# Half of the first shift of an adaLN block: summed on VectorE over transposed rows instead of on TensorE

## The reference

```python
def rms_norm(x, g):
    y = xf * lax.rsqrt(jnp.mean(xf * xf, axis=-1, keepdims=True) + NORM_EPS)
    return (y * g.astype(jnp.float32)).astype(x.dtype)

def adaln(cond, w, b):
    return jnp.split(jax.nn.silu(cond) @ w + b, 6, axis=-1)

def modulate(h, shift, scale):
    return h * (1 + scale) + shift

mx = adaln(cond_x, ada_w[i], ada_b[i])
mc = adaln(cond_c, ada_w[i], ada_b[i])
hx = modulate(rms_norm(x, norm1_g[i]), mx[0], mx[1])
hc = modulate(rms_norm(h_ctx, norm1_g[i]), mc[0], mc[1])
```

## Time and profile before

| | |
|---|---|
| median of 3 timed runs | 1277.91 us |
| the three runs | 1277.8, 1277.91, 1280.22 us |
| span of the profiled execution | 1280.4 us (no other time of it is given) |
| TensorE busy | 1187.3 us, 93% |
| VectorE busy | 744.2 us, 58% |
| ScalarE busy | 510.0 us, 40% |
| POOL busy | 410.8 us, 32% |
| mean granted clock of TensorE | 0.952 |

### The profile page before, as it was taken

The page is one execution under the profiler, slowest core; times in us unless marked ns, Lnnn a source line. Parts: engine busy times, 40 slices in busy tenths (PEclk is TensorE's granted clock), DMA queues, the critical chain, the costliest instruction groups (busy, mean ns, idle before and its releaser), DMA issues.

```text
span 1280.4 us, 17087 instructions
## 1 busy us (share of the span) xinstructions
PE 1187.3 (93%) x6196; PEld 945.7 (74%) x6196; DVE 744.2 (58%) x1082; ACT 510.0 (40%) x858; POOL 410.8 (32%) x185
## 2 busy tenths in 40 slices
PE   6889889897999999999998999997889898999999
PEld 1468653375788888778886788897556587999999
DVE  1688885557598889844114222244467765655544
ACT  2623433533423222322223445463756434544433
POOL 0243210032465555654442433474744200000000
PEclk9889987898999999999998999997989889999999
DMA  9353441033355555654332232343100035455566
GB/s 367 149 187 132 148 132 50 1 110 121 104 192 183 194 185 177 211 171 164 91 101 66 83 98 83 98 164 100 50 1 1 1 103 161 155 190 181 172 180 176
DMA packets 50874, 167.44 MB, mean 131 GB/s; under 512 B 5248, under 2 KB 6400, under 8 KB 50560
## 3 DMA queue, kind: packets, MB, share of 16 engines
q1 hardware_dynamic: 50816, 166.67, 39.7%
HBM read 165.60 MB, written 1.05 MB: 130 GB/s over the span
## 4 chain that ended last, share of the span: by engine, by line
PE 34%; issue 31%; POOL 18%; DVE 10%; DMA 3%; ACT 2%; POOLq 0%; SPq 0%; DVEq 0%; ACTq 0%
POOL wlo L774 18%; PE bank L1253 17%; DVE junk L828 4%; PE bank L1448 2%; PE bank L1262 2%; PE bank L1243 2%; PE bank L1567 2%; PE bank L1556 1%; PE bank L1275 1%; PE bank L1423 1%; DMA xT<-in_x_in 1%; PE bank L1336 1%; PE bank L1651 1%; PE bank L1603 1%; PE bank L1621 1%
## 5 line engine op out<-in xcount | busy, mean ns | idle before, releaser
L774 POOL TENSOR_TENSOR wlo<-raw,whi 128x1024 fp32r<-128x1024 f32 (+2 forms) x141 | 359.0, 2556 | 544.4 <-ACT whi L465 544.3
L1253 PE MATMUL bank<-hhi,whi 128*128 128x256 f32 (+1 forms) x1128 | 381.1, 338 | 3.1 <-POOL wlo L774 2.4
L1253 PE MATMUL bank<-hlo,whi 128*128 128x256 f32 (+1 forms) x1128 | 377.7, 335 | 0.0
L1253 PE MATMUL bank<-hhi,wlo 128*128 128x256 f32 (+1 forms) x1128 | 376.8, 334 | 0.0
L465 ACT ACTIVATE whi<-raw 128x1024 fp32r<-128x1024 f32 (+2 forms) x231 | 224.8, 980 | 202.1 <-DMA raw<-in_w_fo 91.8
L828 DVE SCALAR_TENSOR_TENSOR junk<-aring,csil 128x1024 f32<-128x1024 f32 x144 | 272.6, 1893 | 21.4 <-DMA aring<-in_ada_t 16.4
L1253 PEld LDWEIGHTS bank<-hhi,whi 128*128 128x128 f32 x1128 | 214.1, 190 | 27.5 <-issue 4.4
L1253 PEld LDWEIGHTS bank<-hhi,wlo 128*128 128x128 f32 x1128 | 212.9, 189 | 24.1
L1253 PEld LDWEIGHTS bank<-hlo,whi 128*128 128x128 f32 x1128 | 212.9, 189 | 22.2
L807 DVE TENSOR_TENSOR wlo<-raw,whi 128x1024 fp32r<-128x1024 f32 (+2 forms) x90 | 100.4, 1117 | 88.0 <-ACT whi L465 87.9
L1253 PE MATMUL bank<-ahi,whi 128*128 128x512 f32 (+1 forms) x352 | 118.9, 338 | 1.3 <-DVE scr L920 1.3
(11 more groups left out here) (191 smaller groups left out, 1457.7 us busy)
## 6 DMA issues: line engine op xcount, KB each, us to landing
raw<-in_w_fi SPq DMA_DIRECT2D x88, 512.0 KB, 3.7
aring<-in_ada_t SPq DMA_DIRECT2D x80, 512.0 KB, 3.8
raw<-in_w_in SPq DMA_DIRECT2D x55, 512.0 KB, 3.8
raw<-in_w_out SPq DMA_DIRECT2D x24, 512.0 KB, 4.3
raw<-in_w_fo SPq DMA_DIRECT2D x32, 384.0 KB, 3.1
raw<-in_w_fo SPq DMA_DIRECT2D x32, 320.0 KB, 3.0
ada<-in_ada_w SPq DMA_DIRECT2D x4, 2048.0 KB, 16.4
xT<-in_x_in SPq DMA_DIRECT2D x1, 2048.0 KB, 17.8
```

The costliest lines, as they stand in the source:

```text
L774: nc.gpsimd.tensor_tensor(wlo[:, s, 0:w], raw[:, s, 0:w], whi[:, s, 0:w].bitcast(F32), ALU.subtract).then_inc(lo_ready, 1)
L1253: ins = mm(dst, w[:, s, j * P:(j + 1) * P], xx[:, k0_ + j], start=first and j == 0 and o == 0, stop=last and j == n - 1 and o == 2)
```

## The change

Three of the four row groups remain on TensorE: both halves of the scale and the low half of the shift. The high half of the shift (512 outputs) is made on VectorE in the manner of the later adaLN units: four tiles `shift_w` of 128 outputs by 1024 inputs are loaded transposed (512 KB each, from a new input `ada_s`), and eight multiply-and-sum instructions, two for each tile, write to `asum[:, 4:8]`. They stand on VectorE's list behind the bias of row 1 and the gain, and before the bias of row 0 and the norm. Since they need the Silu of the conditioning rows, these are loaded right behind x, and ScalarE makes their Silu right behind the squares, before the first row copy. The norm's column sums stand behind group 1 instead of group 2; the high parts of chunks 0 and 1 stand behind the last row copy instead of before it. `add_bias` now takes the column of the bias and the number of tiles.

```diff
@@ the sync queue @@
-            for n in range(4):
+            for n in range(3):
                 src = ada_w[1 - n // 2, :, (n % 2) * 512:(n % 2 + 1) * 512].rearrange("(k p) n -> p k n", p=P)
                 sp.dma_start(ada0[:, n], src).then_inc(ada0_in[n], 16)
...
                 if n == 1:
                     sp.dma_start(xT[:, :, :], x_in).then_inc(x_landed, 16)
+                    sp.dma_start(csil[:, :, :], crow).then_inc(crow_in, 16)
+            for t in range(4):
+                sp.dma_start(shift_w[:, t, :], ada_s[t]).then_inc(shift_in[t], 16)
...
-            sp.dma_start(csil[:, :, :], crow).then_inc(crow_in, 16)
@@ ScalarE @@
-            for n in range(4):
+            act.wait_ge(crow_in, 16)
+            nc.scalar.activation(csil[:, :, :], csil[:, :, :], ACT.Silu).then_inc(crow_silu, 1)
+            for n in range(3):
                 act.wait_ge(ada0_rows, n + 1)
                 nc.scalar.activation(rows0[0:2, n, :], bank[n][0:2, :], ACT.Copy).then_inc(rows_out, 1)
-                if n == 2:
+                if n == 1:
                     norm_std(0, HALVES)
-                    act.wait_ge(crow_in, 16)
-                    nc.scalar.activation(csil[:, :, :], csil[:, :, :], ACT.Silu).then_inc(crow_silu, 1)
-                    hi(0)
-                    hi(1)
+            hi(0)
+            hi(1)
             norm(0, HALVES)
@@ VectorE @@
             norm_rstd(0, HALVES)
-            for n, row in enumerate((1, 0)):
-                dve.wait_ge(ada0_sum, n + 1)
-                add_bias(mod[:, row], bank[4 + n][:, 0:16].rearrange("p (k c) -> p k c", c=2), row)\
-                    .then_inc(mods_ready, 1)
-            gains(0, 2)
+            dve.wait_ge(ada0_sum, 1)
+            add_bias(mod[:, 1], bank[4][:, 0:16].rearrange("p (k c) -> p k c", c=2), PV_ADAB + KT, KT)\
+                .then_inc(mods_ready, 1)
+            gains(0, 1)
+            dve.wait_ge(crow_silu, 1)
+            for t in range(4):
+                dve.wait_ge(shift_in[t], 16)
+                for c in range(2):
+                    n = 2 * t + c
+                    if n:
+                        dve.wait_ge(shift_dot, n)
+                    vec.scalar_tensor_tensor(out=junk[:, :], in0=shift_w[:, t, :], scalar=1.0, in1=csil[:, c, :],
+                                             op0=ALU.mult, op1=ALU.mult, accum_out=asum[:, 4 + t, c:c + 1])\
+                        .then_inc(shift_dot, 1)
+            dve.wait_ge(ada0_sum, 2)
+            add_bias(mod[:, 0, 0:4], bank[5][:, 0:8].rearrange("p (k c) -> p k c", c=2), PV_ADAB, 4)
+            dve.wait_ge(shift_dot, 8)
+            add_bias(mod[:, 0, 4:8], asum[:, 4:8, :], PV_ADAB + 4, 4).then_inc(mods_ready, 1)
             norm(0, HALVES)
@@ TensorE @@
-                if n % 2:
+                if n:
                     ins.then_inc(ada0_sum, 1)
 
-            for n in range(4):
+            for n in range(3):
                 pe.wait_ge(ada0_in[n], 16)
...
                 if n:
                     turn_rows(n - 1)
-                if n == 2:
+                if n == 1:
                     norm_total(0, ALL)
-                if n == 3:
-                    norm_turn(0, ALL)
-            turn_rows(3)
+            norm_turn(0, ALL)
+            turn_rows(2)
```

More of the change, by code:

```diff
@@ L142, in conv_taps, with build @@
     return [PV_CW + tap * 24 + tile for tap in range(3)]
-def build(nc, x_in, consts, consts0, pvec, crow, ada_w, ada_t, w_in0, w_out0, w_fi, w_fo, w_in1, w_out1, out):
+def build(nc, x_in, consts, consts0, pvec, crow, ada_w, ada_s, ada_t, w_in0, w_out0, w_fi, w_fo, w_in1, w_out1, out):
     with ExitStack() as ctx:
@@ L193, in build @@
         k0 = over("k0", r_arena, ARENA - A_W, [P, A_W])
-        ada0 = over("ada0", r_arena, 0, [P, 4, KT, 512])
+        ada0 = over("ada0", r_arena, 0, [P, 3, KT, 512])
+        shift_w = over("shift_w", r_arena, 3 * KT * 512, [P, 4, D])
         rows0 = over("rows0", r_arena, 4 * KT * 512, [P, 4, 512])
@@ L265, in build @@
         ada0_sum = sem("ada0_sum")
+        shift_in = [sem(f"shift_in{i}") for i in range(4)]
+        shift_dot = sem("shift_dot")
         ada_used = sem("ada_used")
@@ L808, in lo, with add_bias @@
                                   ALU.subtract).then_inc(lo_ready, 1)
-            def add_bias(dst, src, row, per=0, i=None):
-                b = pv[:, bass.ds(at(PV_ADAB + row * KT, per * KT, i), KT)]
-                b = b.rearrange("p (a n) -> p a n", n=1).broadcast_to([P, KT, dst.shape[2]])
+            def add_bias(dst, src, col, n, per=0, i=None):
+                b = pv[:, bass.ds(at(col, per, i), n)]
+                b = b.rearrange("p (a n) -> p a n", n=1).broadcast_to([P, n, dst.shape[2]])
                 return vec.tensor_tensor(dst, src, b, ALU.add)
@@ L837, in ada_step @@
                     dst = mod[:, bass.ds(at(row, per // KT, i), 1)].rearrange("p a k c -> p (a k) c")
-                    add_bias(dst[:, :, c], asum[:, :, c], row, per // KT, i).then_inc(mods_ready, 1)
+                    add_bias(dst[:, :, c], asum[:, :, c], PV_ADAB + row * KT, KT, per, i).then_inc(mods_ready, 1)
             def gains(k, mods):
@@ L1388, in _ @@
                 if s == 0:
-                    pe.wait_ge(rows_out, 4)
+                    pe.wait_ge(rows_out, 3)
                     two_chunks([bank[0][:, :], bank[1][:, :]], C_IN0, hhi, hlo,
@@ L1736 @@
     ada_t = np.ascontiguousarray(ada_w[2:].transpose(0, 2, 1)).reshape(10 * KT, P, D)
+    ada_s = ada_w[0, :, 512:].T.reshape(4, P, D)
     ada_w = ada_w[:2]
@@ L1750 @@
     x_in = cat([a["ctx"][0], a["x"][0]], axis=0).T.reshape(KT, P, T).transpose(1, 0, 2)
-    arrays = {"x_in": x_in, "consts": k, "consts0": k0, "pvec": pvec, "crow": crow, "ada_w": ada_w, "ada_t": ada_t,
+    arrays = {"x_in": x_in, "consts": k, "consts0": k0, "pvec": pvec, "crow": crow, "ada_w": ada_w, "ada_s": ada_s, "ada_t": ada_t,
               "w_in0": w_in0,
```

## The result

The changed kernel takes 1288.39 us (median of 6 runs, 1285.88 to 1290.25) against 1277.95 before (6 runs, 1277.57 to 1280.22). The ratio is 1.0078, 95% interval 1.0067 to 1.0089: slower by 10 us. The profiled execution took 1288.41 and its span is 1286.6, so the span leaves out 1.8 us.

The account below looks back on a forecast made before the run. TensorE, 93% busy, bounds the kernel; the first norm's start measures the change. Third group's end at 39.3 plus 15.7 gives 55.0 against 45.81, 9.2 us later: 1287.1 us, range 1283.0 to 1290.0.

Parts of the forecast that it names:

- The order on VectorE: VectorE before the first norm: the eight sums stand behind the scale's bias add, so none starts before the third group ends.
- The rival in which the sums run in VectorE's wait: VectorE before the third group's end: sums run there, norm starts 3.1 us earlier than before, time 1274.8; chance 0.03.
- A sum at 1.22 us, 1.27 apart: Eight VectorE sums before the norm: each takes 1.22 us, 1.27 from start to start, 10.2 us for eight.
- Twice that: VectorE sums: by the skill page's half-throughput rule they take double, 9.8 us more, time 1296.9; chance 0.02.
- Two splits, 4.1 us: POOL's splits of chunks 0 and 1 amid VectorE's sums: each costs VectorE 2.07 us, two cost 4.1.
- the lower bound: First norm's start if POOL's splits hold no sum: E + 11.5.
- The Silu, 1.8 us: ScalarE ahead of the first row copy: Silu holds it 1.81 us, moving TensorE's first turn from 27.23 to 29.04.
- The clock: TensorE after its 3.9 us gap: clock falls to 1.2 GHz, 3.6 to 5.3 us at half rate, 1.9 us lost.
- E: End of TensorE's third row group: 39.3 forecast, 37.4 if the clock stays full, 40.0 at most.
- E + 15.7: First norm's start on VectorE: 15.7 us after the third row group ends, after sums, splits and bias adds.
- Nothing later gives it back: Stages behind the first norm: each later wait hangs on this norm, so the 9.2 us delay stays to the end.
- a shrinking distance: Two traces behind the first norm: the prediction would be wrong if their 9 us distance shrank in later stages.

Follow-up runs that it names:

- splits early: Changed kernel, but ScalarE makes the high parts of chunks 0 and 1 as soon as loaded, before the last row copy: 1286.49 us, ratio 1.0059.
- norm's sums moved: Kernel before, with only the norm's column sums moved behind the second row group instead of the third: one profiled execution, 1281.91 us.
- Silu behind: Changed kernel, but the Silu of the condition rows stands behind the copies of rows 0 and 1 on ScalarE: 1286.08 us, ratio 1.0060.
- gap filled: Changed kernel, but TensorE repeats half a row group into an unused bank in its gap ahead of the first turn: 1285.19 us, ratio 1.0048.
- all but place: Changed kernel with Silu behind row copies 0 and 1, a quarter row group filling TensorE's gap, high parts early; sums left in place: 1284.03 us, ratio 1.0038.
- sums ahead: Changed kernel with one block moved on VectorE: the eight sums stand before the scale's bias and the gain: 1279.05 us, ratio 0.9999.
- no sums: Changed kernel without the eight sums; a memset fills asum instead: 1276.07 us, ratio 0.9983.
- sums first, splits held: Changed kernel with Silu behind row copies, sums also ahead of the norm's reciprocal, high parts of chunks 0 and 1 held until sums end: 1279.43 us, ratio 0.9998.
- two tiles: Against changed kernel: two tiles (four sums, early) on VectorE, 256 outputs on TensorE as half-width group, Silu behind row copies, high parts early: 1274.48 us, ratio 0.9967.

## Why the prediction was right

The time came out at 1288.4 for 1287.1 forecast, the ratio 1.0078 for 1.0072. Step by step, at the norm's start: 55.0 forecast, 55.41 found. The steps are right in kind; that the sum came so near is in part luck, since an error of 1.4 us in the clock's term met 0.9 us of errors the other way.

- **The order on VectorE.** Right, and it decides: moving that one block took the ratio from 1.0078 to 0.9999. The rival in which the sums run in VectorE's wait (1274.8) came true when the code was changed to it, but without the 3 us that I gave it: POOL's splits hold the gain and a bias add there, 4.1 us together.
- **A sum at 1.22 us, 1.27 apart.** Right in all runs, wherever no split stood beside it. Twice that, as the Trainium skill would have it on top of the row (Vector Engine (DVE) Microarchitecture Reference, section "Points that are easy to get wrong"), did not happen.
- **Two splits, 4.1 us.** Found 2.02 and 1.95 more for the two long sums, 4.0; in the run with the splits early, where no sum is held, the norm came 11.1 us behind the third group instead of 15.1, where the lower bound had 11.5. That the long sums come from the splits is now shown by moving the splits. The Trainium skill says that the two take turns in SBUF — State Buffer, section "SBUF: two separate sides": an instruction of VectorE with two SBUF inputs and one of GpSimd that reads SBUF go for one port pair by an exclusive lock, and the second to come is blocked for the whole instruction. The traces agree down to the small ones: beside a split a gain of 16 elements took 2.10, a bias add with both inputs in SBUF 1.18 and 2.29, and one from PSUM 0.17.
- **The Silu, 1.8 us.** Right: the turn came at 28.70 where x had landed 0.3 earlier than before.
- **The clock.** Right in kind, small in size. I took 1.9 us from a low stretch of 3.6 to 5.3; it lasted from about 29.3 to 36.1. The third group took 9.79 instead of 7.03 and the norm's small sums ahead of it 1.61 instead of 1.05, 3.3 in all, so E was 40.34 instead of 39.3 and beyond my "40.0 at most". This is the term that was mis-sized; the 0.6 of the next step and the 0.3 by which x landed earlier make up for two thirds of it. Where the size went wrong can be seen in the kernel before: I counted its low stretch from the first projection matmul to the end of my window, 5.3 us, but it began at 47.2, in the gap, and lasted to 54.05, 6.8 us, as long as the one here:

```profile
47.00:47.50 0.50, 0.00 (x0) 0.00 (x0) 0.47 (x2) 0.50 (x2) 0.00 (x0) 0.72 0.00 0
47.50:54.00 6.50, 5.31 (x13) 4.18 (x14) 6.20 (x15) 3.65 (x9) 0.00 (x0) 0.50 0.01 3
54.00:54.50 0.50, 0.50 (x4) 0.41 (x3) 0.50 (x3) 0.00 (x0) 0.00 (x0) 0.95 0.00 0
```

There 1.5 us of it fell on a standing TensorE. I had the clock fall 3.1 us into the new gap as well; it fell after the gap, and the whole stretch was paid at half rate: half of 6.8 is 3.4. For my other source, the first 32 row matmuls, the profile grants 1.00 throughout; only their spacing speaks for a low clock there (5 of them in 9.42 to 13.00, 28 in the 12.1 us behind).

- **E + 15.7** was E + 15.1: the bias adds at the end took 0.2 of my 0.6, the splits 0.1 less, and the first sum started at E + 0.7 instead of 0.8.
- **Nothing later gives it back.** Shown up to 572 us by the two traces. Behind that the traces come nearer to each other by 3 us with another granted clock; the medians don't. I had named a shrinking distance as a sign of being wrong, and by the letter it appeared: 6.2 us at the end. What it tells is less, since the profiled execution before was 4.3 us above its median; that no later stage gives anything back rests on the medians, 10.4 us apart (10.0 by the ratio).

The first projection matmul, read in one execution of each kernel, forecasts the medians of the kernels within 2.3 us. Its shift against before, and the median's by the ratio (times 1278); the run with the norm's sums moved has no median:

| kernel | shift of the first matmul | by the ratio |
|---|---|---|
| changed | +9.6 | +10.0 |
| Silu behind | +6.5 | +7.7 |
| splits early | +5.3 | +7.5 |
| gap filled | +7.0 | +6.1 |
| all but place | +5.0 | +4.9 |
| sums ahead | +1.3 | -0.1 |
| no sums | -1.6 | -2.2 |
| sums first, splits held | -1.8 | -0.3 |
| two tiles | -5.0 | -4.2 |

## What to carry to other kernels

Work that is moved to an idle engine is free only from the point in that engine's list at which it may start: ask what the instruction ahead of it waits for, not how idle the engine is on average. Then count how much fits into the wait: here four sums of 1.22 us were done 1 us before the scale was ready, and eight outlasted the third group by 2.4 us. Ask also which other engine's work it will meet, and whether the engine that feeds the critical one has got a longer list (a Silu of 1.8 us ahead of a copy of 0.5).

## What the runs showed of the hardware

TensorE's clock fell after a gap as short as 2.40 us (with 2.11 it had stayed), in part only when TensorE had been at work again for 0.6 to 2.3 us. It then stayed low from 29.4 to 32.8 in the run with the Silu behind, from 29.3 to 36.1 in the changed kernel. Filling the gap with 3.6 us of matmuls whose result nobody reads brought the norm 2.6 us forward. And a VectorE instruction of 8 elements with both inputs in SBUF took 2.29 us beside a POOL subtraction, where the same add with one input in PSUM took 0.17.
